# Second mixer's sixteen passes: the cosine product goes back to its PSUM bank, the rotation sums read it there, and they and the attention scales change their place in VectorE's order

## The reference, cut to what matters

```
lam_bar = exp(lam * dt)                         # complex, 32 groups x 64 states
bu = einsum('bsgh,gph->bsgp', u, b_bar)         # complex inputs of the states
states = scan over tokens: s = lam_bar * s + bu
y = einsum('bsgp,ghp->bsgh', states, c).real + d_skip * u
...
p = masked_softmax(q k / 8); o = p v            # attention, 8 heads
```

## Time and profile before

| | |
|---|---|
| three runs | 1380.29 to 1381.17 us, median 1380.78 |
| profiled execution, whole | 1380.33 us |
| its span | 1378.6 us |
| PE, DVE, ACT, POOL busy | 1357.8, 1144.3, 780.9, 151.2 us |
| share of the chain that ended last | PE 91%, DVE 4%, ACT 2%, POOL 1%, issue 1% |
| granted TensorE clock | full in every slice |
| mean transfer from HBM and to it | 194 GB/s |

### The profile page before, as it was taken

The page is one execution under the profiler, slowest core; times in us unless marked ns, Lnnn a source line. Parts: engine busy times, 40 slices in busy tenths (PEclk is TensorE's granted clock), DMA queues, the critical chain, the costliest instruction groups (busy, mean ns, idle before and its releaser), DMA issues.

```text
span 1378.6 us, 24203 instructions
## 1 busy us (share of the span) xinstructions
PE 1357.8 (98%) x8485; PEld 1234.1 (90%) x8485; DVE 1144.3 (83%) x1823; ACT 780.9 (57%) x1266; POOL 151.2 (11%) x148
## 2 busy tenths in 40 slices
PE   8999999999999999999999999999999999999999
PEld 7999989989999899998998999989887899889998
DVE  5888877988888888887798999988899977688886
ACT  6444465774444744446577767667554565464442
POOL 0000006200000000000620000025034500000000
PEclk9999999999999999999999999999999999999999
DMA  8766655457666666665556677756634456556662
GB/s 333 232 200 198 201 167 169 158 181 226 200 201 197 227 231 198 199 203 163 171 161 203 224 234 232 227 176 207 222 123 142 122 182 198 184 195 206 196 209 80
DMA packets 73090, 268.05 MB, mean 194 GB/s; under 512 B 8240, under 2 KB 8240, under 8 KB 72752
## 3 DMA queue, kind: packets, MB, share of 16 engines
q1 hardware_dynamic: 69984, 253.79, 57.9%
q10 hardware_dynamic: 3024, 13.15, 2.7%
HBM read 262.71 MB, written 4.19 MB: 194 GB/s over the span
## 4 chain that ended last, share of the span: by engine, by line
PE 91%; DVE 4%; ACT 2%; issue 1%; POOL 1%; DMA 0%; ACTq 0%; DVEq 0%
PE work L793 25%; PE work L794 13%; PE acc L505 9%; PE acc L507 9%; PE acc L506 9%; PE work L505 7%; PE work L507 7%; PE work L506 6%; PE acc L1566 1%; DVE wlo L479 1%; DVE xboth L567 1%; ACT xboth L559 1%; PE work L1538 1%; PE acc L1602 0%; PE work L1059 0%
## 5 line engine op out<-in xcount | busy, mean ns | idle before, releaser
L472 ACT ACTIVATE whi<-raw 128x1024 fp32r<-128x1024 f32 x480 | 495.2, 1047 | 369.6 <-PE work L794 205.7
L479 DVE TENSOR_TENSOR wlo<-raw,whi 128x1024 fp32r<-128x1024 f32 (+1 forms) x460 | 555.2, 1233 | 37.1 <-ACT whi L472 35.8
L793 PE MATMUL work<-xboth,whi 128*128 128x512 f32 x1600 | 530.1, 382 | 0.2
L794 PE MATMUL work<-xboth,wlo 128*128 128x256 f32 x1600 | 436.2, 273 | 0.0
L793 PEld LDWEIGHTS work<-xboth,whi 128*128 128x128 f32 x1600 | 302.4, 189 | 42.9 <-DVE wlo L479 0.9
L794 PEld LDWEIGHTS work<-xboth,wlo 128*128 128x128 f32 x1600 | 306.9, 192 | 2.4
L505 PE MATMUL acc<-whi,hhi 128*128 128x512 f32 x440 | 167.1, 380 | 0.0
L507 PE MATMUL acc<-whi,hlo 128*128 128x512 f32 x440 | 166.8, 379 | 0.0
L506 PE MATMUL acc<-wlo,hhi 128*128 128x512 f32 x440 | 166.8, 379 | 0.0
L505 PE MATMUL work<-xboth,whi 128*128 128x256 f32 (+1 forms) x424 | 118.6, 280 | 0.0
L507 PE MATMUL work<-xboth,wlo 128*128 128x256 f32 (+1 forms) x424 | 117.8, 278 | 0.0
(11 more groups left out here) (463 smaller groups left out, 2095.8 us busy)
## 6 DMA issues: line engine op xcount, KB each, us to landing
raw<-stream SPq DMA_DIRECT2D x480, 512.0 KB, 4.3
par<-pm ACTq DMA_DIRECT2D x2, 1644.5 KB, 7.0
spilled<-rotated ACTq DMA_DIRECT2D x6, 512.0 KB, 5.8
pfa<-pf_a ACTq DMA_DIRECT2D x3, 516.0 KB, 3.7
table<-spilled ACTq DMA_DIRECT2D x3, 512.0 KB, 3.3
par<-spilled ACTq DMA_DIRECT2D x3, 512.0 KB, 3.2
pfb<-pf_b ACTq DMA_DIRECT2D x2, 516.0 KB, 8.1
x<-x_in SPq DMA_DIRECT2D x2, 512.0 KB, 5.7
```

The lines of the kernel that those rows point to most:

```text
L472: nc.scalar.activation(chunk(whi, place, c)[:, cols], chunk(raw, place, c)[:, cols], ACT.Copy).then_inc(hi_ready, 1)
L479: nc.vector.tensor_tensor(chunk(wlo, place, c)[:, cols], chunk(raw, place, c)[:, cols], chunk(whi, place, c)[:, cols].bitcast(F32), ALU.su ...
L793: nc.tensor.matmul(o[:, :], hi[:, k * P:(k + 1) * P], xboth[:, k, :].rearrange("p (h a n) -> p h n a", h=2, a=2), start=k == 0, stop=False)
L794: m = nc.tensor.matmul(o[:, 0:S], lo[:, k * P:(k + 1) * P], woven(xhi[:, k, :]), start=False, stop=k == KD - 1)
```

## The change

Four edits, all in VectorE's order within the second mixer's passes:

1. the sine product comes first, and the cosine product is written to the PSUM bank it reads from and no longer to `sg`;
2. the rotation sums read that bank (one operand in PSUM, one in SBUF) and stand in `front`, behind the products, thus ahead of the convolution and the chunk subtraction; they stood behind these, at the head of the next iteration;
3. the bank of the state inputs counts as emptied after the second sum; before, after the second product;
4. `scales_of` stands behind the chunk subtraction and no longer between the scans and `front`. The title does not name this one; the diff has it.

```
                 b4 = bank2(f"bu{r}").rearrange("p (b n a) -> p b a n", b=2, a=2)
-                step(tt(sg[:, :, :].rearrange("p b (a n) -> p b a n", a=2), b4, cosr, ALU.mult))
-                emptied(f"bu{r}", tt(h32[:, :, :].rearrange("p b (a n) -> p b a n", a=2), b4, sinr, ALU.mult))
+                step(tt(h32[:, :, :].rearrange("p b (a n) -> p b a n", a=2), b4, sinr, ALU.mult))
+                step(tt(b4, b4, cosr, ALU.mult))
+                tt(halved(v2[:, 0, :]), b4[:, 0], halved(h32[:, 1, :]), ALU.add)
+                emptied(f"bu{r}", tt(halved(v2[:, 1, :]), b4[:, 1], halved(h32[:, 0, :]), ALU.subtract))
...
                 vec2.wait(dve, BY_DVE2.index(f"bu{r}") + 1)
-                tt(v2[:, 0, :], sg[:, 0, :], h32[:, 1, :], ALU.add)
-                step(tt(v2[:, 1, :], sg[:, 1, :], h32[:, 0, :], ALU.subtract))
                 if r:
                     rot_ready.wait(dve, r)
...
-                if r % 4 == 2 and r > 2:
-                    scales_of(r // 4 - 1)
                 if r + 1 < ROUNDS:
                     front(r + 1)
...
                 split_lo(dve, place, SPLIT_AFTER[r])
+                if r % 4 == 2 and r > 2:
+                    scales_of(r // 4 - 1)
```

## The result

| | before | changed |
|---|---|---|
| time, median | 1380.91 us (1380.25 to 1381.17, 6 runs) | 1394.6 us (1390.44 to 1395.76, 6 runs) |
| ratio | | 1.0096, 95% interval 1.0086 to 1.0106 |
| profiled execution | 1380.33 us, span 1378.6 | 1393.39 us, span 1391.7 |

The change makes the kernel 13.7 us slower. The forecast was 1387.2 us, with a range up to 1390.5: the sign is right, the size is half, and the time is above the range. The runs also lie further apart (5.3 us against 0.9), in the order of their mean granted clock: 0.998 with 1390.44 us, 0.995 with 1393.39, 0.992 with 1395.76.

What follows compares the result with a forecast made beforehand. TensorE's chain was taken as the bound: three stalls of 3.25 us for late scales (9.75) less 3.3 of waits given back make 6.45 later, 1386.8 us profiled or 1387.2 as median; range 1383 to 1390.5.

Steps and rivals of the forecast that it cites:

- Bound, and the road through ScalarE: TensorE bounds; late scales delay ScalarE's exponentials, which TensorE awaits without slack: 3.25 us at three places, 9.75 in all.
- Rival A: The scales don't decide TensorE's start at `scores(12)`; only its waits for GpSimd shrink: 1377.5 us, chance 0.08.
- rival B: The 3.25 us delay of the scales is paid once, not three times: 1380.8 us, no change, chance 0.07.
- The costs of the edits in PSUM: On VectorE, the cosine product written to PSUM takes 0.71 us; sums reading PSUM cost nothing more than from SBUF.
- Rival C: VectorE's cosine product in its own PSUM bank costs 0.54 us more each time: 1390 us, chance 0.10.
- Rival E: The moved sums on VectorE still stand for GpSimd, growing by about 1 us; inside the range, no chance of its own.
- What came back: TensorE's waits for GpSimd at `states_out` shrink by 1.3, 0.98 and 0.97 us, together 3.3.
- The room of one microsecond: From `scores(12)` to `states_out`, VectorE needs 16.2 us against TensorE's 17.2, so the wait there goes fully.
- the upper bound of 1388.9: Top of the forecast's own bounds, 1385.3 to 1388.9 us, before the range was widened for rivals.
- The clock: TensorE's granted clock taken as full (2.4 GHz) through the stage, with waits up to 1.57 us; no term in the sum.
- rival D: TensorE's clock falls in the stalls, each costing up to 6 us more: up to 1405, likelier a third; chance 0.05.
- What would show it: Expected signs: three TensorE waits of some 3.2 us on ScalarE, ScalarE's scale wait near 20, VectorE under 92%, full clock.

Runs made afterwards that it cites:

- experiment 1: Changed kernel with the scales put back between the scans and the next `front`, other edits kept: 1377.54 us, ratio to before 0.9976.
- experiment 3: Changed kernel plus 26 unused matmuls on TensorE before each of `scores(8)`, `scores(12)` and `turn(15)`, filling its stalls: 1387.92 us, ratio to before 1.0053.
- experiments 1 and 4: The first is experiment 1; the other is the changed kernel with the scales directly behind the second sum, ahead of the chunk subtraction: 1386.14 us, ratio to before 1.0041.
- experiment 8: As experiment 1, but in pass 10 alone the scales stand behind the chunk subtraction: 1382.20 us, ratio to before 1.0011.
- experiment 7: As experiment 1, with pass 0's convolution and subtraction behind pass 1's scans, and pass 2's subtraction ahead of its convolution: 1377.59 us, ratio to before 0.9978.

## Why the prediction was wrong

The medians of four versions split the loss, and the profile's split can be held against them: experiment 1 is 3.2 under before (in the table 3.55 less 0.41), experiment 3 is 10.4 above experiment 1 (10.10), the changed kernel is 6.7 above experiment 3 (6.09). That the three make up the whole is no proof, since they are differences in a row; that each agrees with its part, to 0.6 us at worst, is. And experiment 3 is the changed kernel without the falls of the clock: it took 1387.9 us, where the forecast, which had none, said 1387.2.

*Bound, and the road through ScalarE: right.* The scales were on TensorE's road with no slack, three times. Laid out were 3.87 us, 3.82 of them from the first product to the end of the scales, where pass 10 shows 3.87; the stall was put at 3.25 and moved TensorE by 3.37, three times 10.1 instead of 9.75. Rival A is excluded by experiments 1 and 4, rival B by the three stalls and experiment 8. One size beside this road was wrong and cost nothing: the bank of the state inputs comes free not 1.4 us later but 0.8, counted from the first product (0.71 + 0.69 before, 1074.08 - 1071.86 = 2.22 now).

*The costs of the edits in PSUM: right.* The product written in its own bank took 0.70 (0.71 taken), the sums from PSUM 0.42 and less. Rival C, 0.54 more for each product, didn't come. Nor did the longer fixed part that the Trainium skill gives for a PSUM source ("VectorE: DVE Perf Modes", The TRN2 errata) show: a sum from PSUM takes as long as one from SBUF. Rival E is excluded by the sums beside GpSimd.

*What came back: right in sum.* Forecast 1.3, 0.98 and 0.97; measured 1.46, 1.05 and 1.04. This isn't owed to a slower TensorE behind the stalls: with the clock full, in experiment 3, the wait of pass 2 is again the only one left at `states_out`. The room of one microsecond was added up a tenth short (its terms give 16.1, not 16.2), and the upper bound of 1388.9 two tenths high (1388.7); neither matters. Not foreseen was the 0.35 lost in pass 4. Pass 2's subtraction makes the low parts of the weights of `states_in(3)`, and it starts at 1020.33 rather than 1019.57, since the sums are in front of it. It ends at 1021.56, and `states_in(3)` starts at 1021.70 instead of 1021.38. In experiment 7, which put it ahead of the convolution, it ends at 1021.55 and `states_in(3)` follows the scores at 1022.12 without a gap; but that experiment changed two things. It is the loss of a moved instruction again, only small.

*The clock: wrong, and this is the step that failed.* The sum has no term for it, and rival D stood at 0.05. The argument was that the clock is full in the stage "with waits up to 1.57 in it". That row says nothing of stalls of 3.25: the forecast itself put TensorE into three of them, twice as long as any wait of the stage, and then costed what follows at the clock of the rows without them. The trace of before has one longer idle time, outside the stage, and the forecast didn't look there: TensorE stands 4.64 us at the program's start, and the eight products behind it take 1.94 us, where the same line takes 1.04 later on.

```profile
4.64 1.94 PE L697 MATMUL work<-ident,x 128*128 128x128 f32 x8 [4.64 <-DMA x<-x_in]
...
1198.77 1.04 PE L697 MATMUL work<-ident,x 128*128 128x128 f32 x8
```

The clock column reads 1.00 there, so these two rows are a hint at the price of an idle TensorE and no proof.

Measured are 1.64, 1.63 and 2.82 us behind the three, 6.1 in the profile and 6.7 by experiment 3. What the forecast said of D, that more likely a third of 18 us would come, was the right size; the chance was what failed, and with it the term of the sum. With the clock priced in, the forecast's own numbers would have given 1387.2 + 6 = 1393.2. And since the clock isn't the same in each run, the range had to be wider than a sum of durations makes it.

*What would show it.* The forecast named the clock as a thing by which it would be wrong, and that is what the window row says (0.96). The rest held: three waits of 3.26, 3.26 and 3.35, ScalarE's wait for the scales 19.6 (near 20), `L1566` on GpSimd 1.0 (about 1.3), VectorE under 92%, no sum from PSUM over 0.42, no chunk subtraction over 1.33 between 1000 and 1105 us. Only VectorE's idle time stands mostly elsewhere, before the row maxima for the scores (15.3 us) and not before the first products (1.2).

*What stays open*: why the clock falls behind a stall of 2.73 or 2.12 and not behind one of 2.46 or again 2.12, and why it stayed down longer at the third stall.

## What to carry to other kernels

An instruction of 0.2 us that looks like filler on a busy engine can be the start of another engine's road to the bound; before it is moved behind something, follow who waits for its result, and count the slack to the bound engine's next start, here 0.06 us. A stall that a change puts on TensorE costs more than its length: if it is longer than any in the stage before, the clock at which the work behind it runs is not known from that stage's rows, and needs a term in the sum; the rest of the trace may hold a longer idle time, with the work behind it to compare. Two edits that help each other (an operand in PSUM, an earlier place) can each be worth nothing alone, so undoing one part measures what it is worth beside the others, and not what it would bring by itself.

## What the runs showed of the hardware

- TensorE's granted clock fell to 0.50 in or behind each of the four profiled stalls of 3.26 to 3.35 us, behind one of three of 2.46 to 2.73, and behind one of three of 2.12 to 2.22. Behind the waits of 0.97 to 1.61 us of the kernel before it read 1.00. A fall cost 1.6 to 2.8 us by the profile, and 1.3 by the medians of experiment 8.
- The falls are not the same in each run: the changed kernel's runs spread over 5.3 us, those of the version with filled stalls over 0.9.
- VectorE's product of 128x512 takes 0.70 us when it reads and writes the same PSUM bank, and 0.69 to SBUF. A sum of 128x256 with one input in PSUM takes 0.42 beside a working GpSimd; with both in SBUF it took 1.18 beside it (0.42 without).
